# Dilated attention's projections in nine equal units, issued inside the RWKV passes and inside the first half's softmax steps

## What is computed

```
proj = n @ w_in                                  # n: 512 x 1024
p_r, p_k, p_v, p_wd, p_ad, p_gd, q, k, v, gate_r, gate_a = split(proj)
y_rwkv = rwkv7_mix(p_r, p_k, p_v, ...)           # 16 heads of 64, a scan over the tokens
y_attn = dilated_mixture(q, k, v)                # 12 heads of 64
merged = sigmoid(gate_r) * (y_rwkv @ p_rwkv) + sigmoid(gate_a) * (y_attn @ p_attn)

def dilated_mixture(q, k, v):                    # windows (128,1), (512,4), (2048,16), 4 heads each
    for each group: s = q k^T / 8 - slope * distance, masked to the window and the dilation
                    o, lse = softmax(s) v, logsumexp(s)
    return sum over the groups of softmax(lse over the groups) * o
```

## Time and profile before

| what | value |
|---|---|
| median of 3 runs | 3225.89 us (3225.21 to 3230.78) |
| the profiled execution's own time | 3228.37 us |
| its span in the profile | 3226.6 us |
| mean granted TensorE clock | 0.931 |
| PE / DVE / ACT / POOL busy | 88% / 51% / 20% / 5% |
| chain that ended last, by engine | PE 83%, DVE 9%, issue 4%, ACT 2% |
| RWKV passes | 1568 to 2104 us of the span |
| dilated attention | 2104 to 2379 us |

### The profile page before, as it was taken

One profiled execution on the slowest core, in us unless ns is written; L12 is line 12 of the kernel. 1 busy time (PEld: TensorE's weight loads), 2 busy tenths in 40 slices (PEclk: granted clock), 3 DMA queues, 4 the chain that ended last, 5 costly groups with the idle time before them and its releaser, 6 DMA issues.

```text
span 3226.6 us, 44375 instructions
## 1 busy us (share of the span) xinstructions
PE 2855.0 (88%) x17389; PEld 2074.8 (64%) x17389; DVE 1630.8 (51%) x2182; ACT 648.1 (20%) x1104; POOL 176.4 (5%) x203
## 2 busy tenths in 40 slices
PE   5799667999989999999888989787879988889998
PEld 3455443888868778886455555553547776668886
DVE  6677663444455554444456655412145463365554
ACT  3133311211010121101323222212121121121011
POOL 2000210000000000001200011000000000000000
PEclk8899778999999999999999999897889989999999
DMA  6376102233323323332101001030113222223331
GB/s 224 112 248 202 43 0 65 87 96 93 98 77 98 91 78 96 91 96 64 37 23 29 23 23 38 15 91 28 45 35 92 86 85 62 62 79 93 96 98 65
DMA packets 406152, 255.25 MB, mean 79 GB/s; under 512 B 23864, under 2 KB 391057, under 8 KB 405905
## 3 DMA queue, kind: packets, MB, share of 16 engines
q1 hardware_dynamic: 402432, 243.63, 25.7%
q0 software_dynamic: 2320, 5.11, 0.5%
q10 hardware_dynamic: 1280, 4.78, 0.4%
HBM read 250.60 MB, written 2.10 MB: 78 GB/s over the span
## 4 chain that ended last, share of the span: by engine, by line
PE 83%; DVE 9%; issue 4%; ACT 2%; DMA 0%; DVEq 0%; ACTq 0%; POOL 0%; SPq 0%; POOLq 0%
PE PS L712 13%; PE PS L713 13%; PE PS L714 13%; PE PS L699 7%; PE PS L1368 5%; PE PS L727 3%; PE PS L728 3%; PE PS L729 3%; PE PS L1135 3%; PE PS L1545 1%; PE PS L1537 1%; PE PS L1443 1%; PE PS L1411 1%; PE PS L1441 1%; PE PS L1562 1%
## 5 line engine op out<-in xcount | busy, mean ns | idle before, releaser
L738 DVE CAST WH<-W 128x1024 fp32r<-128x1024 f32 x304 | 210.8, 694 | 721.5 <-PE PS L714 549.3
L740 DVE TENSOR_TENSOR WL<-W,WH 128x1024 fp32r<-128x1024 f32 x304 | 372.6, 1226 | 10.4
L713 PE MATMUL PS<-XNL,WH 128*128 128x512 f32 x864 | 343.3, 397 | 0.0
L712 PE MATMUL PS<-XNH,WH 128*128 128x512 f32 x704 | 277.3, 394 | 0.0
L714 PE MATMUL PS<-XNH,WL 128*128 128x512 f32 x704 | 275.4, 391 | 0.0
L714 PE MATMUL PS<-HH,WL 128*128 128x512 f32 x672 | 261.5, 389 | 0.0
L713 PE MATMUL PS<-HL,WH 128*128 128x512 f32 x672 | 261.5, 389 | 0.0
L712 PE MATMUL PS<-HH,WH 128*128 128x512 f32 x672 | 261.4, 389 | 0.0
L727 PE MATMUL PS<-XNH,WH 128*128 128x512 f32 x448 | 180.4, 403 | 32.7 <-DVE XNL L671 32.6
L728 PE MATMUL PS<-XNL,WH 128*128 128x512 f32 x480 | 194.5, 405 | 0.0
L699 PE MATMUL PS<-HXF,W 128*128 128x512 f32 (+2 forms) x384 | 170.0, 603 | 20.4 <-ACT HXF L632 7.1
(11 more groups left out here) (464 smaller groups left out, 4691.5 us busy)
## 6 DMA issues: line engine op xcount, KB each, us to landing
ARENA<-in_ada_w SPq DMA_DIRECT2D x80, 512.0 KB, 5.0
W<-in_ffn_w SPq DMA_DIRECT2D x64, 512.0 KB, 4.0
W<-in_w_in SPq DMA_DIRECT2D x58, 512.0 KB, 3.9
W<-in_ffn_w_gate SPq DMA_DIRECT2D x44, 512.0 KB, 3.8
W<-in_ffn_w_up SPq DMA_DIRECT2D x44, 512.0 KB, 3.8
W<-in_ffn_w_down SPq DMA_DIRECT2D x32, 512.0 KB, 4.2
W<-in_sc_w_in SPq DMA_DIRECT2D x24, 512.0 KB, 3.8
W<-in_ada_w SPq DMA_DIRECT2D x16, 512.0 KB, 4.8
```

Of the source, the lines that this page charges most:

```text
L712: nc.tensor.matmul(dst, WH[:, h, c], hi(k), start=(start and k == 0), stop=False)
L713: nc.tensor.matmul(dst, WH[:, h, c], lo(k), start=False, stop=False)
L738: nc.vector.tensor_copy(WH[:, h, :], W[:, s, 0:D]).then_inc(parted, 1)
L740: nc.vector.tensor_tensor(WL[:, h, :], W[:, s, 0:D], WH[:, h, :], ALU.subtract).then_inc(freed[s], 1)
```

## The change

The projections of a half are now nine units of the same size, q, k and v of each of the three groups, each 128 columns of weights. The six for q and k are eight matmuls 128x512 as before (`dilated_product`); the three for v are 32 matmuls 128x128 each, four in the place of one of the eight (`dilated_tokens`). All write bank 7, and ACT copies each to its own tile (`DIL0`, `DIL1`).

- The first half's unit i goes into ahead pass i: one matmul in each of the last four steps of the state chain, one before `y`, one before the mean, two before the variance. ACT copies it after the two exponentials (step `dil`), and the next pass's projection 0 waits for that copy. Units 7 and 8 go into the eighth pass: 7 in place of projection 0, 8 within the levels.
- So that bank 7 is free, projection 2 moves from the state chain into the levels, one matmul before and one after each `xz` of levels 1 to 4, and the gate's two matmuls move from level 2 to behind `w`. ACT's order follows: projection 1's copy before the `akv` copy, projection 2's before the `w` copies, the gate's after them.
- The second half's units go into the first half's steps: unit 0 after `scores(0)`, then unit s+1 in step s, three matmuls before the transposes, then two, two and one behind each of the three groups. ACT copies unit s+1 at the end of step s, ahead of the exponential of step s+1.
- The weights of the first half's units lie in the unused thirds of the ring's slots (two slots to a unit, double-buffered, `dw_in`, `dw_used`); the second half's come through the ring.
- The factor 1/8 moves from ACT's copy of q into DVE's bias step (`stt` in the place of `tt`). The transposes use three banks by turns (3, 4, 6) instead of four. The first bias tables are loaded before the eighth pass; the second half's one by one as each is free. The memory tokens and some tiles lie elsewhere. The loops over passes on SP and ACT and over halves on all engines are written out.

```diff
-            steps["act"] = (next_pair("raw0") + "tr0 tr1 tr2 tr3 "
...
+            steps["act"] = (("raw0" if ahead else "dila") + " tr0 tr1 tr2 tr3 "
...
+                            + (" raw2 " if ahead else " dil ") + "w0 w1 gg yp" + next_pair("sw aa") + "csq" + next_pair("e1 en dil") + "groot")
...
+            def dil_weights(u):
+
+                b = u % 2
+                if u > 1:
+                    sp.wait_ge(dw_used[b], u // 2)
+                for j in range(2):
+                    nc.sync.dma_start(w_tail(b, j), w_cols(w, AT_Q + 2 * P * u)[:, 4 * j:4 * j + 4, :]).then_inc(dw_in[b], 16)
...
+            def dilated_product(u, k, w):
+
+                return nc.tensor.matmul(bank[7], w, xn(k), start=(k == 0), stop=(k == KD - 1))
+
+            def dilated_tokens(step, w):
+
+                t, ks = step // 2, range(step % 2 * 4, step % 2 * 4 + 4)
+                for k in ks:
+                    mm = nc.tensor.matmul(bank[7][:, t * P:(t + 1) * P], XN[:, k, t * P:(t + 1) * P], w(k), start=(k == 0), stop=(k == KD - 1))
+                return mm
...
+                if ahead:
+                    early = lambda ks: projection(2, ks, "raw1")
+                    late = lambda ks: dilated(i, ks, "gg")
+                else:
+                    early = lambda ks: dilated(8, ks, "dila")
+                    late = lambda ks: None
...
+                    if step == "before":
+                        pe.wait_ge(rw_act.sem, rw_act.before("dil", i))
...
+                    if l:
+                        early(range(2 * l - 2, 2 * l - 1))
...
+                    if l:
+                        early(range(2 * l - 1, 2 * l))
...
-                if ahead:
-                    projection(2, range(0, 3), p_act, "gg")
...
-                    if ahead and 3 <= c < 6:
-                        projection(2, range(c + 2, c + 3), p_act, "gg")
+                    if c >= 3:
+                        late(range(c - 3, c - 2))
...
+                late(range(4, 5))
                 pe.wait_ge(p_dve.sem, p_dve.done("s6", at))
...
+                late(range(5, 6))
                 pe.wait_ge(p_dve.sem, p_dve.done("ys", at))
                 nc.tensor.matmul(bank[0], PAIR_ONES, YS, start=True, stop=True).then_inc(p_pe.sem, p_pe.step("mean"))
+                late(range(6, KD))
...
                 scores(0)
+                fill(0, range(KD))
                 for s in range(8):
                     if s < 7:
                         scores(s + 1)
                     if s == 4:
                         values(0)
-                    turn(s)
+                    fill(s + 1, range(0, 3))
+                    for g in range(NG):
+                        turn(s, g)
+                        fill(s + 1, (range(3, 5), range(5, 7), range(7, KD))[g])
                 values(1)
...
+                if ahead:
                     decays(at, p_act, p_dve)
+                    dilated_out(i, i // 2 + 1, p_act, "dil")
```

More of the change, by code:

```diff
@@ L45 @@
 GATE_R, GATE_A = 5664, 6688
+DIL_UNITS = 9
 DIL_GROUPS = ((128, 1), (512, 4), (2048, 16))
@@ L875, in _ @@
+            pair_weights("rw_first", 0, 0)
+            dil_weights(0)
+            dil_weights(1)
+            for i in range(RW_PAIRS - 1):
+                pair_weights("rw", i, i + 1, i + 1 if i else None)
+            dil_weights(RW_PAIRS - 1 + 1)
+            for u in range(DIL_UNITS):
+                s = ring.slot("dil", u)
+                sp.wait_ge(freed[s], ring.free("dil", u))
+                nc.sync.dma_start(tiles(s), w_cols(w, AT_Q + 2 * P * u + P)).then_inc(landed[s], 16)
             with sp.Fori(0, KD) as i:
@@ L1402, in pair_pass @@
                 if ahead:
-                    projection(1, range(0, 5), p_act, "raw0")
+                    projection(1, range(0, 5), "raw0")
                 for l in levels:
@@ L1459, in pair_pass @@
                 mm.then_inc(p_pe.sem, p_pe.step("w"))
-                if ahead:
-                    projection(2, range(3, 5), p_act, "gg")
+                bank_read("raw2" if ahead else "dil")
+                lora, n = W[:, ring.slot("rw", 3), :], GATE_LORA - P
+                nc.tensor.matmul(bank[7], lora[:, P:2 * P], GD0, start=True, stop=False)
+                nc.tensor.matmul(bank[7], lora[0:n, 2 * P:3 * P], GD1[0:n, :], start=False, stop=True).then_inc(freed[ring.slot("rw", 3)], 1)
                 pe.wait_ge(p_act.sem, p_act.done("w1", at))
@@ new lines, in scores, with turn @@
+                    mm.then_inc(dl_pe[half].sem, dl_pe[half].step(f"s{s}"))
+                def turn(s, g):
+                    if g == 0:
+                        pe.wait_ge(dl_dve[half].sem, dl_dve[half].done(f"p{s}"))
+                    before = 24 * half + NG * s + g - 3
+                    if before >= 0:
+                        own = dl_act[before // 24]
+                        pe.wait_ge(own.sem, own.done(f"t{before % 24 // NG}{before % NG}"))
+                    for c in range(s % 4 + 1):
+                        mm = nc.tensor.transpose(bank[DL_TURN[g]][:, c * P:(c + 1) * P], SD[:, s % 2, g, c * P:(c + 1) * P], IDENT)
+                    mm.then_inc(dl_pe[half].sem, dl_pe[half].step(f"t{s}{g}"))
@@ L1931, in pair_pass @@
                     nc.scalar.activation(W21[:, 4 * e:4 * e + 4, :, :].rearrange("p n w d -> p (n w d)"), bank[e], ACT.Copy).then_inc(p_act.sem, p_act.step(f"w{e}"))
-                if ahead:
-                    raw("rw", 2, i, 7, p_act)
+                act.wait_ge(freed[ring.slot("rw", 3)], ring.free("rw", 3, i))
+                nc.scalar.activation(GG, bank[7], ACT.Copy).then_inc(p_act.sem, p_act.step("gg"))
                 act.wait_ge(p_pe.sem, p_pe.done("yp", at))
```

275 lines of the change are left out of this document (136 added, 139 removed).

## The result

| | before | after |
|---|---|---|
| median | 3227.78 us (4 runs) | **3145.0 us** (3141.83 to 3156.24, 4 runs) |
| ratio to before, 95% interval | | **0.9752** [0.9736, 0.9768] |
| profiled execution / span | 3228.37 / 3226.6 us | 3146.47 / 3144.6 us |
| mean granted TensorE clock | 0.931 | 0.941 |
| PE busy | 88% | 90% |

What follows compares the result with a forecast made beforehand. No engine is full in the softmax, where PE waits at clock 0.65; in passes PE is busy 60.8 of 67.7 us. 3228.37 - 93.9 (halves) + 28.2 (passes) = 3162.7 us profiled, median 3160, range 3136 to 3188.

Steps and rivals of the forecast that it cites:

- First half: First half's softmax with the second half's nine units in it: PE work 104.7 us plus 3 of waits, 107.7 us.
- the interruption: In the first half, each break in a unit's matmuls adds 0.2 us; 32 of them cost 6.4 us.
- The waits: PE's remaining waits in the first half, for DVE's scaling steps and ACT's last copy: 3 us in all.
- v units: Units of 32 matmuls of 128 columns: 0.23 us a matmul, 7.4 us a unit (7.0 to 10.5).
- Rival 5: Narrow v matmuls don't hide their weight loads: 192 matmuls cost 0.37 us more each, +71, total 3231 us; chance 0.02.
- Second half: The second half's softmax, without units, keeps its chain and stays at 73.25 us.
- Bank 7: In the passes, the next projection 0 waits for ACT's copy of the unit: +1.8 us, six times, 10.8.
- The levels: In the passes' levels, projection 2's matmuls come in and the gate's leave; the 3.6 us balance fills waits: 0.
- From `w` to the mean: End of a pass, with gate matmuls, later key norm and two single unit matmuls: +2.0 us, seven times, 14.0.
- Eighth pass: Unit 7 +1.0, unit 8 in the levels +1.5, the gate behind `w` +0.9: together +3.4 us.
- Weights at nothing: Loading the units' and decay weights in the passes costs 0 us; they are needed some 13 us later.
- Rivals 1 to 4: Gaps absorb units: 3140, 0.07; PE bounds passes: 3207, 0.08; weights late: 3195, 0.05; first half at half clock: 3265, 0.03.

Runs made afterwards that it cites:

- run 1: The changed kernel with all nine units of the second half issued ahead of the first half's softmax steps: 3186.2 us, ratio to before 0.9881.
- run 6: The changed kernel with each second-half unit in one piece ahead of the step's transposes instead of four pieces around them: 3148.34 us, ratio to before 0.9756.
- run 2: The changed kernel with the first half's nine units behind the eighth pass instead of inside the passes: 3192.09 us, ratio to before 0.9892.
- run 5: The changed kernel with ACT's copy of the first half's unit ahead of the two exponentials instead of behind: 3139.62 us, ratio to before 0.9726.
- run 4: The kernel before with two extra 512-column matmuls between mean and variance of each ahead pass, result overwritten: 3218.75 us, ratio to before 0.9976.
- run 3: The kernel before with only ACT's loop over the seven passes written out: 3218.88 us, ratio to before 0.9975.

## Why the prediction was right, and which of its terms were not

The sum gave 3162.7 us for the profiled execution, which took 3146.5. The difference of 16.2 is made of: first half -5.2, second half -1.9, passes -5.7, the stages ahead and behind, which I had at nothing, -2.6 and -0.9. These parts are read from single profiles; of the medians, 3160 was forecast and 3145.0 measured. Some of the 15 us is scatter: the passes alone differ by 9.8 us between profiles of the same work (538.7 to 548.5 us).

- **First half, 107.7 predicted, 102.5 measured; clock about 1.0 predicted, 0.98 measured.** The mechanism is as written, and run 1 shows it by taking it away. The mis-sized term is the interruption: 32 x 0.2 = 6.4 us. It came from a single matmul between 64-row tiles; between 128x128 transposes it is near nothing (run 6). I carried a price from one neighbourhood to another. The waits, 3 us predicted, are about 1. Against both stands a cost that I had left out: PE enters the half after 6.55 us of idling, so unit 0 and the first scores take 2.1 us longer (run 2).
- **v units, 7.4 predicted, 7.25 measured.** Rival 5 is refuted. In the stretch of the row of weight loads 192 of them took 192 ns each, 36.9 us in all, within some 22 us of matmuls of the same form (three units), and were under way during 22.4 us, so they overlap one another as well. The Trainium skill, in "TensorE: Matmul & The Clock Gate", section "The mechanism" (under "What overlaps and what doesn't"), says that a load overlaps matmuls in flight only where the row group differs. By an estimate from it a unit would take 32 x (0.22 + 2 x 0.19) = 19 us; this case's trace disagrees with it for float32 at 128 columns as it did at 192 and 512.
- **Second half, 73.25 predicted, 71.4 measured.** Its own work did not change, but it is no constant: the profiles show 68.5 us (run 1), 69.5 (run 6), 74.9 (run 5) and 75.0 (run 2) for the same work, since parts of it run at either clock level. In after, `values` at its end took 8.50 us where 9.46 stood before, and PE's wait for DVE's scaling is shorter by 0.08 to 0.16 us in each step that has one (2.98 instead of 3.14 in steps 2 and 6). I put that down to the loop over halves being written out; that wasn't tried by itself.
- **The factor 1/8 in DVE's bias step, nothing predicted.** The widest takes 1.76 us, as in the earlier trace rows:

```profile
2245.61 1.76 DVE L2650 SCALAR_TENSOR_TENSOR ARENA<-PS,ARENA 128x1536 f32<-128x1536 f32 x1 [5.80 <-PE PS L1583]
```

- **Bank 7, +1.8 a pass predicted, +1.3 measured** (5.42 less 4.1 on average). The prediction took ACT to reach its square 0.2 us sooner; it reached it 0.6 sooner, because the table load moved ahead of the wait. I read the order rows of ACT at the exponentials, where a REGISTER_ALU vanished and no wait stood, and not at the sigmoids, where the load crossed a wait.
- **The levels, 0 predicted, +0.2 measured** against a pass whose projection 0 was warm: 49.33 - 5.42 = 43.9 us from projection 0 to `w`, before 47.70 - 4.03 = 43.7.
- **A term missing: the cold projection 0**, partly at the lower clock. I wrote that the two matmuls before the variance cost nothing. They gain: four of six passes had lost some 1.7 us there (run 4). Over six passes about -7 us, so mean to `w` grew by 0.5 a pass and not by 1.8.
- **From `w` to the mean, +2.0 predicted, +1.9 measured.** Right on average; single values go from 18.30 to 21.49 us, by the clock:

```profile
1751.70:1770.00 18.30, 16.53 (x290) 10.47 (x290) 11.19 (x17) 5.03 (x8) 0.00 (x0) 1.00 0.37 96
1819.30:1840.80 21.50, 19.73 (x290) 12.28 (x290) 11.22 (x17) 5.01 (x8) 0.00 (x0) 0.84 0.32 82
```

The same instructions, 1.00 and 0.84: 3.2 us.
- **Eighth pass, +3.4 predicted, +5.1 measured.** Behind `w` the period grew by 0.9 (14.15 to 15.02), as predicted for the gate. The miss lies between the mean and `w`: +4.3 (42.20 to 46.47) where units 7 and 8 were put at +2.5. I counted the bank's wait six times, and unit 7 waits for it too (1.75 us), but that explains only some 0.5: run 5 takes the wait away and gets no more, since PE then waits longer for DVE. Where the rest goes is not shown.
- **Weights at nothing**: no row of a projection or unit in the passes names a DMA as what it waited for. Rivals 1 to 4 are out: the passes grew by 22.5 (16.0 to 25.7 over the four profiles of these passes), not by 8, 63 or 75, and the clock of the first half rose.

The passes' +28.2 was thus close to +22.5 partly by luck, through cancelling: against the passes of run 2, with the table loaded early and one cold projection 0 instead of four (510.8 us), the units cost 34.5, and 11.7 came back that the prediction did not have. Of the 11.7, 6.3 lie between mean and `w` of six passes, where these two effects are (48.84 to 47.79 on average); the other 5.4 lie in the eighth pass and behind `w` and are not traced to a cause.

## What to carry to other kernels

Independent matmuls put into a stretch where PE waits for a chain through other engines paid twice here, in PE's idle time and in its clock. Such a stretch should not be left empty while another is full: three of nine units moved to the still empty half took 15.9 us off the two halves, where the order of the pieces within a step (run 6) gave nothing. Measure a filler's price in the neighbourhood where it will stand, and read what each engine does before the stretch, since PE may enter it at the lower clock. When a loop is written out, look at every instruction that stands behind a register's wait: here a table load moved ahead of it.

## What the runs showed that I had not expected

- Ahead of the sigmoids the ACT_TABLE_LOAD of 1.28 us stood behind a wait against a register and stands ahead of one against a constant, so writing out one engine's loop is worth 0.25% of this kernel (run 3).
- Two matmuls more in each ahead pass, whose result nobody reads, made the kernel 8 us faster (run 4).
- The second half's softmax, the same instructions, takes 68.5 to 75.0 us from profile to profile, and the `w`-to-mean part of a pass 18.3 to 21.5 us within one profile, the long ones at the lower mean clock.
